# Hybrid encoder step on eight cores: layer 0's v stage, its sample block, and the scheduler's waits and shift transfers

## The reference, cut to what matters

```python
# layer 0 of 4: chunked gMLP; D_MODEL 1024, D_INNER E = 2048
h = rms_norm(x, g_norm[i]) * (1.0 + scale) + shift      # adaLN from the conditioning vector
u, v, z = jnp.split(jnp.einsum('bsd,de->bse', h, w_in_a), 3, axis=-1)
u = jax.nn.gelu(u, approximate=False)
v = layer_norm(jax.nn.gelu(v, approximate=False), ln_a_g, ln_a_b)
y = u * chunk_mlp_mix(v, w_s_a, b_s_a)   # out[i] = sum_j W[g,i,j] v[j] + b[g,i], blocks of 128 rows, 8 head groups
out = jnp.einsum('bse,ed->bsd', y * jax.nn.silu(z), w_out_a)
v_rows = v                               # returned for the sample tokens
# layer 1: gated conv of width 3; layer 2: GLU, depthwise conv of width 31, layer norm; layer 3: pooling
x = x + gate * out
```

## Time and profile before

| what | value |
|---|---|
| median of 3 runs | 2259.24 us (2257.51 to 2262.3) |
| the profiled execution | 2259.4 us |
| its span, slowest core (core 4) | 2257.8 us (cores 2246.2 to 2257.8) |
| TensorE (PE) busy | 2122.4 us, 94% |
| DVE / ACT / POOL busy | 1046.8 / 672.8 / 322.3 us |
| mean granted TensorE clock, core 4 | 0.982 |
| chain that ended last | PE 83%, DMA 6%, DVE 5%, issue 2%, ACT 2%, the rest 2% |
| DMA | 232.43 MB moved, mean 103 GB/s |

### The profile page before, as it was taken

One profiled execution on the slowest core, in us unless ns is written; L12 is line 12 of the kernel. 1 busy time (PEld: TensorE's weight loads), 2 busy tenths in 40 slices (PEclk: granted clock), 3 DMA queues, 4 the chain that ended last, 5 costly groups with the idle time before them and its releaser, 6 DMA issues.

```text
span 2257.8 us, 41011 instructions; the slowest of 8 cores (2246.2 to 2257.8 us)
## 1 busy us (share of the span) xinstructions
PE 2122.4 (94%) x15851; PEld 1320.6 (58%) x15851; DVE 1046.8 (46%) x1482; ACT 672.8 (30%) x861; POOL 322.3 (14%) x593
## 2 busy tenths in 40 slices
PE   4999999998999999999999997999989999999995
PEld 1644666445666666666666564666655566666663
DVE  3444150442555454655545222853326666455535
ACT  3254302543111112111121334613446322213331
POOL 1011101111000100001002441105430000000000
PEclk9999999999999999999999998999999999999997
DMA  9915848058333644346435985549974544344424
GB/s 206 197 32 84 141 71 140 14 92 142 68 68 68 101 71 85 66 75 112 75 68 110 198 184 118 94 75 197 197 166 78 94 73 70 64 75 72 79 43 151
DMA packets 90637, 232.43 MB, mean 103 GB/s; under 512 B 16400, under 2 KB 41616, under 8 KB 90288
## 3 DMA queue, kind: packets, MB, share of 16 engines
q0 software_dynamic: 53264, 181.82, 46.0%
q1 hardware_dynamic: 37184, 48.00, 8.3%
HBM read 339.51 MB, written 9.55 MB: 155 GB/s over the span
## 4 chain that ended last, share of the span: by engine, by line
PE 83%; DMA 6%; DVE 5%; issue 2%; ACT 2%; SPq 1%; POOL 1%; DVEq 0%; ACTq 0%; POOLq 0%
PE ps L461 73%; PE ps L692 5%; DMA tmp<-tmp 2%; DMA ring<-w_in_a 1%; SPq L130 1%; DMA ring<-w_ada 1%; DVE tmp L909 1%; PE ps L953 1%; PE ps L761 1%; PE ps L757 1%; DVE tmp L1023 1%; DMA xa_sb<-xa 0%; PE ps L407 0%; DMA ysT<-tmp 0%; DVE ysT L1038 0%
## 5 line engine op out<-in xcount | busy, mean ns | idle before, releaser
L461 PE MATMUL ps<-hT,ring 128*128 128x352 bf16 (+1 forms) x8448 | 1299.7, 315 | 26.0 <-DVE ysT L768 5.5
L461 PEld LDWEIGHTS ps<-hT,ring 128*128 128x128 bf16 x8448 | 826.0, 98 | 493.3 <-issue 45.5
L461 PE MATMUL ps<-ysT,ring 128*128 128x352 bf16 (+1 forms) x3072 | 468.9, 313 | 10.9 <-DVE xb_sb L550 5.1
L461 PEld LDWEIGHTS ps<-ysT,ring 128*128 128x128 bf16 x3072 | 297.3, 97 | 182.3 <-issue 19.2
L130 POOL DMA_DIRECT2D tmp<-tmp x256 | 129.2, 511 | 129.3 <-DVE histG L915 44.6
L692 PE MATMUL ps<-ring,hT 128*128 128x512 bf16 (+1 forms) x576 | 128.9, 383 | 5.1 <-DMA ring<-w_in_a 3.8
L909 DVE TENSOR_TENSOR tmp<-tmp,ps 128x1074 bf16<-128x1074 f32 (+3 forms) x64 | 45.5, 712 | 170.5 <-issue 83.5
L821 ACT ACTIVATE tmp<-ps 128x1074 f32<-128x1074 f32 (+1 forms) x32 | 33.9, 1059 | 265.3 <-PE ps L461 191.3
L832 DVE TENSOR_TENSOR tmp<-tmp,ps 128x1074 f32<-128x1074 f32 (+3 forms) x64 | 45.4, 709 | 139.4 <-PE ps L461 127.4
L961 ACT ACTIVATE tmp<-ps,cst_sb 128x16 bf16<-128x16 f32 (+2 forms) x160 | 70.0, 437 | 112.8 <-PE ps L953 92.3
L544 DVE SCALAR_TENSOR_TENSOR xb_sb<-ps,modT,xb_sb 128x1056 f32<-128x1056 f32 x32 | 42.2, 1318 | 120.7 <-PE ps L461 120.2
(11 more groups left out here) (154 smaller groups left out, 1691.1 us busy)
## 6 DMA issues: line engine op xcount, KB each, us to landing
ring<-w_in_b POOLq DMA_DIRECT2D x64, 512.0 KB, 6.2
ring<-w_ada POOLq DMA_DIRECT2D x48, 512.0 KB, 9.2
ring<-w_in_a POOLq DMA_DIRECT2D x48, 512.0 KB, 12.4
ring<-w_in_c POOLq DMA_DIRECT2D x48, 512.0 KB, 6.2
ring<-w_in_d POOLq DMA_DIRECT2D x32, 512.0 KB, 5.1
tmp<-tmp SPq DMA_DIRECT2D x128, 69.4 KB, 6.7
tmp<-tmp POOLq DMA_DIRECT2D x128, 69.4 KB, 5.8
tmp<-tmp SPq DMA_DIRECT2D x128, 67.5 KB, 5.9
```

What stands on the lines that cost most here:

```text
L461: ins = h.matmul(PSB[:, 3 * sl + n, 0:W], lhsT=lw, rhs=rh[:, n * W:(n + 1) * W], start=(first and k == 0), stop=(last and k == len(pairs) ...
```

## The change

Eight edits, most of them in layer 0:

1. `_deps` sorts the waits by the time at which what they wait for was recorded, and leaves out those that a later one implies (`at`, `past`: what the awaited instruction's engine had itself seen).
2. A new `dma_group` issues several DMAs on one semaphore. `spread` uses one for SP and one for POOL, `gather` one; the convolution waits for two semaphores and not 16.
3. The bias operands are made on all 128 partitions (four copies of the 32 rows), and a mix issues its four bias matmuls together, each on its own 32 rows, ahead of the sixteen others.
4. The sample block is no longer a block of its own: `sample_front` (32 matmuls on four column groups of bank 2) stands behind block 2, `sample_stats` and `sample_back` stand in the middle of the projections of blocks 4 and 5. Its buffers are `wrep`, `outP[2]` and `histG`.
5. `front` takes the v weight tiles one after the other (bank by bank) and frees each at once in the last block; it can begin at bank 4.
6. `load_b` moves from hook 4 to the v stage of group 0, without marking a read of `ys.7`; `wrep` is loaded in layer 1.
7. The adaLN part (1, 2) moves from hook 3 to hook 5.
8. After the last mix the slot is set so that z tile 1 takes banks 0 to 2; `vrows` is made with fewer, smaller operations.

```diff
+        seen = self.seen[eng]
+        todo = sorted(((a, v) for a, v in waits.items() if seen.get(a, 0) < v), key=lambda e: self.at[e])
         out = []
-        for sname, v in waits.items():
-            if self.seen[eng].get(sname, 0) >= v:
+        for n in range(len(todo) - 1, -1, -1):
+            a, v = todo[n]
+            if seen.get(a, 0) >= v:
                 continue
-            self.seen[eng][sname] = v
-            out.append((sname, v))
+            out.insert(0, todo[n])
+            for b, w in self.past[todo[n]].items():
+                if w > seen.get(b, 0):
+                    seen[b] = w
+            seen[a] = max(v, seen.get(a, 0))
         return out
...
+    def dma_group(self, parts, reads=(), writes=()):
+        waits = [self._deps(q, reads, list(writes) + list(own)) for q, _, _, own in parts]
+        for (q, slot, moves, own), wl in zip(parts, waits):
...
+            self.cnt[slot] += 16 * len(moves)
...
+                for out, in_ in moves:
+                    h.dma_start(out=out, in_=in_).then_inc(dsm, 16)
...
-        bb, bs = tf(0, 2048)[0:32, :], tf(2048, 1024)[0:32, :]
...
+        bb, bs = tf(0, 2048), tf(2048, 1024)
...
+        s.dma("sp", "su_lb", bb, ln_a_gb[1:2, :].rearrange("a n -> (a n)").partition_broadcast(128), writes=tk(0, 2048))
...
+    BBS = 2048
+    outb = outP[2].rearrange("p a b -> p (a b)").bitcast(BF16)
+    gvs, vns, wrs = wrep.bitcast(F32), outb[:, 0:512], v3(outb[:, 512:576], 2)
...
+    def sample_weights():
+        for q in range(4):
+            s.dma("sp", "su_wss%d" % q, w32s[32 * q:32 * q + 32, :, :], ws_d.rearrange("p (a i) -> p a i", a=8)[0:32, 2 * q:2 * q + 2, 0:32],
+                  writes=["wss%d" % q])
...
-            blocks = [dict(hc=128 * i, oc=128 * i, no=128, w0=0, n=128, smp=0) for i in range(8)]
-            blocks += [dict(hc=NPA, oc=NPA, no=32, w0=0, n=32, smp=1)]
+            blocks = [dict(hc=128 * i, oc=128 * i, no=128, w0=0, n=128) for i in range(8)]
...
+        first_bank = 4 if rr["i"] == 0 else 0
+
+        def front(bi, mid=None):
...
+            for nq in range(4):
+                if nq == 2 and mid:
+                    mid()
                 for kh in range(2):
...
+                            ins = h.matmul(PSB[0:n, b0 + nq, :], lhsT=hT[:, kh * 4 + kk, hc:hc + n], rhs=vw[nq * 2 + kh][:, kk, :],
+                                           start=(kh == 0 and kk == 0), stop=(kh == 1 and kk == 3))
...
+                    if bi == nb - 1:
+                        release(vspec[nq * 2 + kh])
...
+        def sample_front():
+            def f(h):
+                ins = None
+                for kc in range(8):
+                    for nq in range(4):
+                        ins = h.matmul(PSB[32 * nq:32 * nq + 32, 2, :], lhsT=hT[:, kc, NPA:NPA + 32], rhs=vw[nq * 2 + kc // 4][:, kc % 4, :],
+                                       start=(kc == 0), stop=(kc == 7), skip_group_check=True)
+                return ins
...
+        def sample_stats():
...
+            s.op("pe", lambda h: h.matmul(PSB[:, 7, 0:2], lhsT=qsum, rhs=stat[:, SO:SO + 2], start=True, stop=True), reads=k + ["qsum"], writes=bk(7))
...
+            s.op("pool", lambda h: h.tensor_tensor(out=st(6), in0=st(5), in1=stat[:, 20:21], op=ALU.pow), reads=k + ["neghalf"], writes=rk)
+            for q in range(4):
...
+                s.op("dve", lambda h, q=q, r=r: h.scalar_tensor_tensor(out=vns[r, :], in0=gvs[r, :], scalar=stat[r, SO + 3:SO + 4],
+                                                                       in1=gbc[r, 512 * q:512 * q + 512], op0=ALU.subtract, op1=ALU.mult),
+                     reads=k + ["wrep"] + tk(GBC, 2048), writes=["vns%d" % q])
+            s.op("act", lambda h: h.activation(out=wrs, in_=w32s, func=AF.Copy, scale=st(6)), reads=WSSK + rk, writes=["wrs"])
...
+        def mix(oc, no, w0, br, body):
...
+                for bank in range(4):
+                    r = 32 * bank
+                    ins = h.matmul(v3(PSB[:, 4 + bank, :], 4)[:, :, 0:no], lhsT=biasL[r:r + 32, bank * 128:(bank + 1) * 128],
+                                   rhs=br[r:r + 32, bank, :, w0:w0 + no], start=True, stop=False, skip_group_check=True)
+                return ins
+            s.op("pe", f_bias, reads=BIASK, writes=bk(4, 5, 6, 7))
+            body()
...
         def vrows_parts():
...
+            ax, ak = tf(BBS, 512), tk(BBS, 512)
...
+            def work():
+                s.op("dve", lambda h: h.tensor_scalar(out=gvs, in0=gvs, scalar1=stat[:, SO + 3:SO + 4], scalar2=stat[:, SO + 6:SO + 7],
+                                                      op0=ALU.subtract, op1=ALU.mult), reads=["wrep", "stS", "rsS"], writes=["wrep"])
...
+                for q in range(4):
+                    s.dma("sp", "o_vr%d" % q, vrows[:, 512 * q:512 * q + 512], gvs[32 * q:32 * q + 32, :], reads=["wrep"], writes=["O.vrows%d" % q])
...
+        mids = {4: sample_stats, 5: sample_back} if g == 1 else {}
         for bi in range(nb):
-            front(bi)
+            front(bi, mids.get(bi))
             if bi:
                 back(bi - 1)
+            if g == 1 and bi == 2:
+                sample_front()
             stats(bi)
+            if g == 0 and bi == 2:
+                load_b()
+                sample_weights()
...
                 if it + ci == 0:
                     back(nb - 1)
+                    rr["i"] = 1
...
+            s.dma_group(parts, reads=tk(GB[ci], 560), writes=tk(RB[ci], 2240) if c < 2 else [])
...
+            s.op("pe", f, reads=["R%d.%d" % (ci, r) for r in range(2)] + tk(RB[ci], 2240) + tk(WD[ci], 512), writes=sk(sl))
...
-        s.dma("pool", "su_wr", wrep, wrep_d, reads=["ys.7"], writes=["wrep"])
         for d in range(8):
-            s.dma("sp", "x1.%d" % d, xt[1][:, d, :], x_in[1][d], reads=["ys.7"], writes=["x1.%d" % d])
+            s.dma("sp", "x1.%d" % d, xt[1][:, d, :], x_in[1][d], after=["st1"], writes=["x1.%d" % d])
+
+    def load_wrep():
+        s.dma("pool", "su_wr", wrep, wrep_d, after=["ys.0"], writes=["wrep"])
...
-    HOOKS = {(0, 0): {0: [mix_bias], 4: [load_b], 10: [(0, 2)], 13: [(1, 0)]},
-             (0, 1): {1: [(1, 1)], 3: [(1, 2)], 11: [(2, 0)], 14: [(2, 1)]},
-             (1, 0): {3: [(2, 2)]},
+    HOOKS = {(0, 0): {0: [mix_bias], 10: [(0, 2)], 13: [(1, 0)]},
+             (0, 1): {1: [(1, 1)], 5: [(1, 2)], 11: [(2, 0)], 14: [(2, 1)]},
+             (1, 0): {0: [load_wrep], 3: [(2, 2)]},
```

More of the change, by code:

```diff
@@ L114, in op, with dma @@
         self._mark(eng, val, reads, writes)
-    def dma(self, q, slot, out, in_, reads=(), writes=(), **kw):
+    def dma(self, q, slot, out, in_, reads=(), writes=(), after=(), **kw):
         if slot not in self.sem:
@@ L119, in dma @@
             self.cnt[slot] = 0
-        waits = self._deps(q, reads, writes)
+        waits = self._deps(q, list(reads) + list(after), writes)
         self.cnt[slot] += 16
@@ L340, in build_program @@
     s.op("dve", f_mask, reads=["ident"], writes=["dmask"])
+    s.op("dve", lambda h: h.tensor_reduce(out=qsum[:, 0:32], in_=ident.rearrange("p (b q) -> p q b", b=4), axis=AX, op=ALU.add), reads=["ident"], writes=["qsum"])
+    for q in range(1, 4):
+        s.op("dve", lambda h, q=q: h.tensor_copy(out=qsum[:, 32 * q:32 * q + 32], in_=qsum[:, 0:32]), reads=["qsum"], writes=["qsum"])
     def ada_mm(l, part, AT):
@@ L748, in vrows_parts @@
[L748 to L764 removed]
+                for q in range(4):
+                    s.dma("sp", "su_ln%d" % q, ax[32 * q:32 * q + 32, :], ln_a_gb[1:2, 512 * q:512 * q + 512].rearrange("a n -> (a n)").partition_broadcast(32),
+                          writes=ak if q == 0 else ["lnb%d" % q])
@@ L769, in back, with sample_back, body, f @@
                      reads=yk, writes=bk(4 + bank) + yk)
+        def sample_back():
+            def body():
+                def f(h):
+                    ins = None
+                    for i in range(4):
+                        for bank in range(4):
+                            r = 32 * bank
+                            ins = h.matmul(v3(PSB[:, 4 + bank, :], 4)[:, i, 0:32], lhsT=vns[r:r + 32, i * 128:(i + 1) * 128], rhs=wrs[r:r + 32, i // 2, :],
+                                           start=False, stop=True, skip_group_check=True)
+                    return ins
+                s.op("pe", f, reads=["vns%d" % q for q in range(4)] + ["wrs"], writes=bk(4, 5, 6, 7))
+            mix(NPA, 32, 0, biasRS, body)
+        def back(bi):
+            b = blocks[bi]
+            n, no, oc, w0 = b["n"], b["no"], b["oc"], b["w0"]
+            def body():
+                for bank in range(4):
+                    def f(h, bank=bank):
+                        ps = v3(PSB[:, 4 + bank, :], 4)
+                        ins = None
+                        for i in range(4):
+                            cc = bank * 4 + i
+                            ins = h.matmul(ps[:, i, 0:no], lhsT=vn[0:n, cc * 128:(cc + 1) * 128], rhs=wr[0:n, cc // 2, w0:w0 + no],
```

(12 more changed lines are left out.)

156 lines of the change are left out of this document (74 added, 82 removed).

## The result

The changed kernel takes **2211.3 us** (median of four runs, or 2210.1 without the one of 2293.4), the kernel before 2260.0 us in the same comparison: ratio 0.978, 95% interval 0.976 to 0.980, 49 to 50 us faster. The forecast was 2215.7. Executions in which some cores ran at a lower granted clock than the rest are left out of every comparison here: whole dies as a rule, two cores each in a run of 2240.8 us of "one row group" and in the profiled run, 2230.7 us, of the table's last kernel, which the ratios with their intervals still contain. The profiled execution took 2208.56 us, with a span of 2207.0 on core 7, its slowest.

The account below looks back on a forecast made before the run. The prediction took TensorE, busy for 94% of the span, to bound the kernel. Savings of 15.9 (group 0), 21.1 (group 1), 6.2 (layer 2) and 0.5 make 43.7, so 2259.4 us becomes 2215.7, range 2204 to 2231.

Parts of the forecast that it names:

- Bias in four row groups: v stage: four bias matmuls run together and cost about one; mix 1.3 us, saving 1.28 us per 128-wide block.
- The short power: v stage: with a wait dropped, POOL's power takes 0.55 us instead of 1.53, 1.1 us earlier per block.
- the rival with the hold: v stage: the power stays long, held behind a DVE operation or by its second wait; period 9.05, 2227 us; chance 0.15.
- Group 0, 15.9: Layer 0, group 0: last v tile, shorter mixes and earlier z tiles together save 15.9 us.
- +5.5: Group 0's v stage: moving the x loads lets the last v tile land in time, saving 5.5 us.
- Group 1, 21.1: Layer 0, group 1: hook move, mixes, sample inserts, stage tail, z tiles and scratch move together save 21.1 us.
- the last v tile is 0 to 2 us late. +1.7: Group 1's v stage: moving the adaLN part to hook 5 removes two waits but delays this tile; net gain 1.7 us.
- Layer 2, 6.2: Layer 2, group 0: grouped shift transfers start L909 1.0 us earlier and remove TensorE's pauses, saving 6.2 us, bounds 0 to 8.
- rival C: Layer 0: late tiles and the sample's inserts collide worse than counted, by 5 to 8 us: 2222 us; chance 0.13.
- rival D: Layer 2: the grouping doesn't bring the gain, since L909's delay is not its waits: 2222 us; chance 0.10.
- B: v stage: the bias matmuls run one behind the other, 0.65 us more each of 13 times: 2224 to 2226; chance 0.07.
- E: z stages: the clock stays at half level behind the longer pauses, 59 us for each stage: 2259 to 2330; chance 0.03.

Follow-up runs that it names:

- Experiment 1: The changed kernel with the four bias matmuls of a full block all reading one row group: 2218.3 us.
- the table's last kernel: The changed kernel with the adaLN part back at hook 3 and the first z tiles issued before the v stage's last power: 2205.0 us.
- experiment 2: The changed kernel with the old list of waits, in no order and nothing pruned: 2228.3 us.
- experiment 3: The kernel before with only the new ordered, pruned waits: 2251.1 us against 2263.2, ratio 0.9946.
- experiment 6: The changed kernel with group 1's x transfers issued at hook 4 again: 2215.9 us.
- experiment 5: The changed kernel with group 1's adaLN part back at hook 3 instead of 5: 2206.5 us.
- the second execution: The changed kernel itself once more, nothing changed, profiled again as a control: median 2211.9 us over four runs.
- experiment 9: The changed kernel without the line that sets the accumulator slot behind the last mix: 2221.4 us.
- experiment 8: The kernel before with layer 0's adaLN scratch moved to a buffer that the vrows transfers don't read: 2251.6 us.
- experiment 4: The changed kernel with one semaphore for each of layer 2's shift transfers again, waits still ordered and pruned: 2218.6 us.
- the two executions with the z tiles first: The changed kernel with the first z tiles issued before the v stage's last power: 2208.4 us; with the adaLN part also at hook 3: 2205.0.

## Why the prediction was right, point by point

The range held the time, and the likeliest case was the right one: both main mechanisms, the row groups and the short power, came as described. That layer 0 comes out at 36.8 us for 37.0 is luck in part, since errors of 1 to 4 us in its terms cancel.

- **Bias in four row groups**: right. Mix 1.23 us for 1.3, period 8.23 for 8.2. Experiment 1 shows that they run together.
- **The short power**: right, the rival with the hold was wrong for this kernel. Power 0.55, in every block but a few, 0.04 behind L801. Without the dropped wait layer 0 pays what the rival had for it (experiment 2). The prediction had one side of how the two parts need each other, row groups without the short power; the other side, that the short power alone gives nothing in the v stage, is experiment 3.
- **Group 0, 15.9**: 14.9. Two errors. "+5.5" for the last v tile was read on the slowest core. Over all eight the first block's excess fell from 3.55 us (2.4 to 5.2) to 0.38, and experiment 6 gives 4.3. Against it, the z stage gave 3.3, not 2.3: z tile 1 starts 2.4 us sooner behind z tile 0, as foreseen, and the 96 matmuls from it on take 16.75 us instead of 17.90, since the shorter pause costs less clock, a gain that no term had; z tile 0 itself is 0.3 slower on average.
- **Group 1, 21.1**: 21.1 to 21.9, by accident. The step that failed is "the last v tile is 0 to 2 us late. +1.7" for the hook: the excess is 4.3 to 5.3 us, and against hook 3 the move costs 4 to 5 us (experiment 5). The rate of 2.7 to 3.2 us a tile was right, 2.9 to 3.3 over the cores. But seven tiles are issued from 15.0 us before the stage on, the first of them lands only 5.0 to 7.0 us later, and with six more the last is there 9.7 us into the stage, 3.7 after it is needed (4.5 in the second execution). The lone tile of the earlier trace rows takes 5.1; a range of 0 to 2 has no room for such a first landing. That part of rival C came. On the other side, "z tile 0 goes slow as in group 0 (+3.05)" was read from one core: it is slow on three of eight, as against two before, and costs 0.2 us more than before on average. The slot was worth 4.6 with its clock (experiment 9) where I had 1.7 and 1.4, and the `vrows` term, 7.1, measured 7.6 (experiment 8). The sample's inserts were right: the steps from block to block that hold them are 10.70, 8.98 and 9.55 us instead of 8.23, together 4.5 for 4.65.
- **Layer 2, 6.2, and "everything else that loses a wait lies under TensorE: +0.5"**: this is the mis-sized sum. Layer 2 gained about 12 to 13 us, group 0 8.8 and group 1 4.3 in the profiled execution. The steady period was as foreseen (0.47 a chunk). Missed were the pipeline's first steps and its end in both groups. By the traces the first steps were held by POOL's wait for SP's first transfer, which the prediction did not see in the diff (experiment 4); no run tests that wait alone. Why the last step fell too, by about 1.2 us in each group, stays open. "Group 1 has no such pause" read only its steady blocks. Of rival D, the part that L909's delay is not its waits is excluded by experiments 2 and 3: it falls from 1.28 us to 0.32 with groups and to 0.18 with the pruned waits. But the grouping isn't needed for it.
- Rivals B and E did not come: the mix is 1.23 us, and the clock was back within the first z tiles.

Sum over layer 0: 36.8 us in the profiled execution, 35.9 in the second, forecast 37.0; layer 2 took the whole excess.

## What to carry to other kernels

Two chains with nearly the same period (9.49 and 9.07 us here) hide each other: of 1.26 us a block, shortening the one through DVE, POOL and ACT gave 0 alone and shortening the one on TensorE 0.42, so price a change against both. A transfer that waits for a ring slot must be priced with everything that is freed at the same moment: the first landing, and then the rate of the queue. Read a term on all cores, since the slowest one has the unluckiest transfers and the clock may be low on a few only; fill and drain of a pipeline deserve their own lines beside its steady period. And when accesses are regrouped, look for waits that go with the old order of marking, not only for merged semaphores.

## What the runs showed of the hardware

- **The power beside the centring.** Over the eight cores, a power that starts 0.04 to 0.05 us behind the start of the two-input DVE operation took 0.55 us in 118 of 120 cases in the changed kernel (114 of 120 in its second execution) and 1.7 in the others, all at 0.05. Those that start 0.16 behind took 1.53 (all 112 in experiment 2), and those at 0.40 took 1.3 (8 in the changed kernel). All of these end about 1.7 us behind the start of an operation that takes 1.27. So the hold is real, and there is a gap of some 0.05 us at its beginning through which a short one slips. The Trainium skill ("SBUF — State Buffer", "Who interferes with whom") has the later one waiting for all of the earlier; the cases from 0.16 on agree. The short ones at 0.04 to 0.05 do not, and there the measurement decides.
- **Satisfied waits cost time.** Sixteen waits for transfers long landed held the DVE product back by 1.28 - 0.18 = 1.1 us, about 0.07 each; with groups and the old waits, fourteen fewer, it starts 0.96 sooner, which is 0.07 each again.
- **Spread within one execution.** The stop for one weight tile ranged from 2.4 to 5.2 us over the cores of the kernel before (the slow clock behind it included), and z tile 0 of group 0 in the changed kernel took 3.84 us on four cores and 5.5 to 6.7 on the other four.
- **Left open**: why layer 2 was 1.5 to 4.7 us longer in the two executions with the z tiles first. The sample block inside the stage, the two row switches instead of eight, and the two effects of grouping were not tried alone.
